# Opening of a diffusion step on one core: modulation weights loaded in column quarters, first five projections run over k in four passes

## What is computed

```
m = silu(cvec) @ w_ada + b_ada            # w_ada is 1024 x 6144, cvec: two vectors (context, latent)
sh1, sc1, g1, sh2, sc2, g2 = split(m, 6)  # each 1024 wide
h = rmsnorm(x) * norm_mix * (1 + sc1) + sh1
p = h @ w_in                              # w_in is 1024 x 3600, split into mq mk mv mo gate dq dk dv
```

## Time and profile before

| | |
|---|---|
| median of 3 runs | 712.12 us (709.15 to 714.17) |
| profiled execution, its own time | 710.51 us |
| its span | 708.6 us |
| PE busy | 663.3 us, 94% |
| DVE, ACT, POOL busy | 52%, 23%, 13% |
| mean granted TensorE clock | 0.982 |
| HBM traffic | 255 GB/s over the span |

### The profile page before, as it was taken

How to read it: one execution, slowest core, us unless ns; L and a number is a source line. 1 busy time by engine, 2 the same in 40 slices (tenths; PEclk the granted TensorE clock), 3 DMA queues, 4 the chain that set the end, 5 groups by cost and what they waited for, 6 DMA issues and landing times.

```text
span 708.6 us, 7606 instructions
## 1 busy us (share of the span) xinstructions
PE 663.3 (94%) x2646; PEld 362.3 (51%) x2646; DVE 368.8 (52%) x748; ACT 160.2 (23%) x416; POOL 95.0 (13%) x120
## 2 busy tenths in 40 slices
PE   3799999999999999999999899996999999999993
PEld 3344474345556555577778654443744444444441
DVE  3315562431465655366645636857563445545477
ACT  6000210001222221136655703222200100000113
POOL 1042100112203201020322310121100000000040
PEclk9899999999999999999999999999999999999997
DMA  7988833913015569999952249414899999999573
GB/s 281 387 261 307 322 136 118 358 31 134 31 30 164 229 274 375 421 352 420 420 239 64 87 159 406 176 70 191 303 341 370 389 344 349 346 370 336 208 296 148
DMA packets 63621, 181.46 MB, mean 256 GB/s; under 512 B 5622, under 2 KB 19310, under 8 KB 59492
## 3 DMA queue, kind: packets, MB, share of 16 engines
q1 hardware_dynamic: 54088, 157.53, 61.1%
q0 software_dynamic: 4384, 12.48, 4.9%
q10 hardware_dynamic: 5116, 11.02, 4.0%
HBM read 122.71 MB, written 58.25 MB: 255 GB/s over the span
## 4 chain that ended last, share of the span: by engine, by line
PE 74%; DVE 8%; DMA 8%; SPq 5%; issue 3%; ACT 1%; ACTq 0%; POOL 0%; DVEq 0%; POOLq 0%
PE PS L1645 24%; PE PS L2050 10%; PE PS L1878 7%; PE PS L1637 5%; PE PS L1793 5%; SPq L529 4%; PE PS L2070 4%; DMA RING<-scratch_xs 3%; PE PS L1865 2%; PE PS L1676 2%; DMA PR<-in_w_ada 2%; DMA PR<-scratch_mod 1%; PE PS L1772 1%; PE PS L1586 1%; PE PS L1822 1%
## 5 line engine op out<-in xcount | busy, mean ns | idle before, releaser
L1645 PE MATMUL PS<-RING,hT 128*128 128x512 f32 x400 | 180.7, 600 | 0.8 <-DVE hT L1053 0.8
L1645 PEld LDWEIGHTS PS<-RING,hT 128*128 128x128 f32 x400 | 73.6, 191 | 86.6 <-issue 85.6
L2050 PE MATMUL PS<-PR,RING 128*128 128x512 f32 x192 | 85.3, 593 | 0.6 <-DVE RING L1424 0.6
L1878 PE MATMUL PS<-RING,hT 128*128 128x512 f32 x160 | 72.7, 600 | 0.0
L2050 PEld LDWEIGHTS PS<-PR,RING 128*128 128x128 f32 x192 | 35.7, 190 | 41.4 <-issue 40.7
L1878 PEld LDWEIGHTS PS<-RING,hT 128*128 128x128 f32 x160 | 29.0, 190 | 30.5 <-issue 30.5
L2070 PE MATMUL PS<-PR,TMP 128*128 128x512 f32 x96 | 43.2, 592 | 0.0
L1793 PE MATMUL PS<-RING,hT 128*128 128x256 f32 x160 | 36.9, 384 | 0.7 <-ACT TMP L860 0.6
L1637 PE MATMUL PS<-hT,RING 128*128 128x512 f32 (+3 forms) x128 | 37.1, 450 | 0.0
L949 ACT ACTIVATE TMP<-PS 128x256 f32<-128x256 f32 x16 | 6.1, 384 | 131.5 <-PE PS L2050 131.5
L1030 DVE TENSOR_TENSOR TMP<-PS,TMP 2x512 f32<-2x512 f32 x24 | 16.4, 682 | 36.8 <-PE PS L1676 32.1
(11 more groups left out here) (345 smaller groups left out, 950.0 us busy)
## 6 DMA issues: line engine op xcount, KB each, us to landing
scratch_xs<-fnorm SPq DMA_DIRECT2D x16, 2560.0 KB, 23.6
PR<-in_w_gate_up SPq DMA_DIRECT2D x12, 2048.0 KB, 19.9
PR<-in_w_ada SPq DMA_DIRECT2D x20, 1024.0 KB, 10.4
RING<-in_w_in SPq DMA_DIRECT2D x14, 1024.0 KB, 7.5
PR<-in_w_down SPq DMA_DIRECT2D x12, 1024.0 KB, 23.3
hT<-in_w_gate_up SPq DMA_DIRECT2D x4, 2048.0 KB, 21.8
RING<-scratch_xs SPq DMA_DIRECT2D x56, 128.0 KB, 15.1
scratch_xs<-RING ACTq DMA_DIRECT2D x14, 512.0 KB, 12.5
```

The source lines that it names most:

```text
L1645: last = mm(PS[:, bank, :], hTv[:, k, t * P:(t + 1) * P], ring[:, ci % 2, k, :], start=(k == 0), stop=(k == KD - 1))
L1878: last = mm(PS[:, i % 4, :], hTv[:, k, t * P:(t + 1) * P], ring[:, (WOUT + q) % 2, k, :], start=(k == 0), stop=(k == KD - 1))
L2050: last = mm(PS[:, 4 + b, :], xgT[:, b, k, :], gub[s][:, k, :], start=(k == 0), stop=(k == KD - 1))
```

## The change

Each of the four modulation chunks now holds 256 columns of shift and the 256 columns of scale that belong to the same features; one chunk is enough to modulate two k blocks. `QUARTER` says which quarter of the features chunk n_ holds (0, 2, 1, 3 for n_ = 0, 1, 2, 3; in the order of PE, chunks 0, 2, 1, 3, the quarters are 0, 1, 2, 3). A transfer of such a chunk is all 8 k blocks by 256 columns. The first half of the mk chunk is loaded before ada 2, the second before ada 3. `modulate1(c)` and `ada_cols(c)` work by quarters, and the first five projections run in four passes of two k blocks (`first_proj`). The other tiles still use `proj` by halves.

```
 load_ada1(n_):
-            for hf in range(2):
-                sp.dma_start(ada_w1[n_][:, 4 * hf:4 * hf + 4, :], w_late[hf, :, :, n_ * 512:(n_ + 1) * 512]
+            c = QUARTER[n_]
+            for s in range(2):
+                sp.dma_start(ada_w1[n_][:, :, 256 * s:256 * s + 256], w_first[:, :, D * s + 256 * c:D * s + 256 * c + 256]
...
         load_ada1(0)
+        load_chunk(0, (0,))
         load_ada1(2)
-        load_chunk(0, (0,))
         load_ada1(1)
+        load_chunk(0, (1,))
         load_ada1(3)
-        load_chunk(0, (1,))
...
-        pool.dma_start(TMP[ROWS4 - 1:ROWS4, 2048:4096], bias[0:2048].unsqueeze(0)).then_inc(early_loaded, 16)
+        for s in range(2):
+            pool.dma_start(adp[ROWS4 - 1:ROWS4, :, 256 * s:256 * s + 256],
+                           bias[D * s:D * s + D].rearrange("(c n) -> c n", c=4).unsqueeze(0)).then_inc(early_loaded, 16)
...
+        def modulate1(c):
+            dve.wait_ge(ada_done, c + 1)
+            V.tensor_copy(adp[0:ROWS4 - 1, c, :], PS[0:ROWS4 - 1, 4, :]).then_inc(ada_row, 1)
+            dve.wait_ge(adacol_T, c + 1)
+            V.tensor_copy(modc[:, 2 * c:2 * c + 2, :], PS[:, 6, 4 * c:4 * c + 4].rearrange("p (k c) -> p k c", c=2))
+            step(V.scalar_tensor_tensor(modc[:, 8 + 2 * c:10 + 2 * c, :], ...
+            if c == 0:
+                dve.wait_ge(hraw_a, NT)
+                dve.wait_ge(hraw_v, NT)
+            for r, (lo, hi) in enumerate(((0, CTX), (CTX, T))):
+                for k in range(2 * c, 2 * c + 2):
+                    V.tensor_scalar(hTv[:, k, lo:hi], hTv[:, k, lo:hi], modc[:, 8 + k, r:r + 1], modc[:, k, r:r + 1],
+                                    ALU.mult, ALU.add).then_inc(h_ready, 1)
...
         ada(0, 0)
         xn_T(4)
-        pe.wait_ge(early_loaded, 48)
-        ada_cols(0, 0)
-        ada(2, 1)
-        ada_cols(2, 1)
+        pe.wait_ge(early_loaded, 64)
+        ada_cols(0)
...
+        def first_proj(m, c):
+            if m < 4 and c == 0:
+                pe.wait_ge(hraw_a, NT)
+                pe.wait_ge(hraw_v, NT)
+            if m == 0 and c % 2 == 0:
+                halves(0, c // 2)
+            for k in range(2 * c, 2 * c + 2):
+                if m < 2:
+                    pe.wait_ge(h_ready, 4 * c + 2 * m + k % 2 + 1)
+                last = mm(PS[:, FIRST_BANK[m], :], hTv[:, k, m * P:(m + 1) * P], ring[:, 0, k, :],
+                          start=(k == 0), stop=(k == KD - 1))
+            if c == 3:
+                last.then_inc(mm_done, 1)
...
-        proj(0, 0)
-        proj(1, 0)
+        for m in range(NT):
+            first_proj(m, 0)
+        ada(2, 1)
+        ada_cols(1)
+        for m in range(3):
+            first_proj(m, 1)
         ada(1, 2)
-        proj(2, 0)
-        ada_cols(1, 2)
+        first_proj(3, 1)
+        first_proj(4, 1)
+        ada_cols(2)
+        for m in range(3):
+            first_proj(m, 2)
         ada(3, 3)
-        proj(3, 0)
-        ada_cols(3, 3)
-        proj(4, 0)
+        first_proj(3, 2)
+        first_proj(4, 2)
+        ada_cols(3)
         for m in range(ALONE * NT):
             w, t = WIN_ORDER[m // NT], m % NT
             if m >= NT:
                 proj(m, 0)
-            proj(m, 1)
+                proj(m, 1)
+            else:
+                first_proj(m, 3)
             if m == 0:
                 gates()
```

More of the change, by code:

```diff
@@ L51 @@
 FIRST_BANK = (2, 3, 0, 1, 5)
+QUARTER = (0, 2, 1, 3)
 ADA2_AT = {4: 1, 5: 2, 6: 3, 7: 8, 8: 9, 9: 10, 10: 11, 11: 12}
@@ L429, in _ @@
             sp.dma_start(x_in[:, t, :], src).then_inc(x_loaded[t], 16)
+        w_first = a["w_ada"][0].rearrange("(k p) n -> p k n", p=P)
         w_late = a["w_ada"][0].rearrange("(h k p) n -> h p k n", h=2, p=P)
@@ L433, in load_ada1 @@
             done = (late_in[0], None, late_in[1], ada3_in)[n_]
-            for hf in range(2):
-                sp.dma_start(ada_w1[n_][:, 4 * hf:4 * hf + 4, :], w_late[hf, :, :, n_ * 512:(n_ + 1) * 512]
-                             ).then_inc(half_in[2 + hf] if n_ == 1 else done, 16)
+            c = QUARTER[n_]
+            for s in range(2):
+                sp.dma_start(ada_w1[n_][:, :, 256 * s:256 * s + 256], w_first[:, :, D * s + 256 * c:D * s + 256 * c + 256]
+                             ).then_inc(half_in[2 + s] if n_ == 1 else done, 16)
         load_ada1(0)
+        load_chunk(0, (0,))
         load_ada1(2)
-        load_chunk(0, (0,))
         load_ada1(1)
+        load_chunk(0, (1,))
         load_ada1(3)
-        load_chunk(0, (1,))
         def load_ada2(n_):
@@ L1035, in ada_rows @@
             last.then_inc(ada_row, 1)
[L1037 to L1048, removed]
+        def modulate1(c):
[3 more added lines that the diff above has]
+            V.tensor_copy(modc[:, 2 * c:2 * c + 2, :], PS[:, 6, 4 * c:4 * c + 4].rearrange("p (k c) -> p k c", c=2))
+            step(V.scalar_tensor_tensor(modc[:, 8 + 2 * c:10 + 2 * c, :],
+                                        PS[:, 6, 16 + 4 * c:20 + 4 * c].rearrange("p (k c) -> p k c", c=2), 1.0,
+                                        cols[:, 16 + 2 * c:18 + 2 * c].unsqueeze(2).broadcast_to([P, 2, 2]), ALU.add, ALU.mult))
+            if c == 0:
                 dve.wait_ge(hraw_a, NT)
                 dve.wait_ge(hraw_v, NT)
-            for c, (lo, hi) in enumerate(((0, CTX), (CTX, T))):
-                for k in range(4 * hf, 4 * hf + 4):
-                    V.tensor_scalar(hTv[:, k, lo:hi], hTv[:, k, lo:hi], modc[:, 8 + k, c:c + 1], modc[:, k, c:c + 1],
+            for r, (lo, hi) in enumerate(((0, CTX), (CTX, T))):
+                for k in range(2 * c, 2 * c + 2):
+                    V.tensor_scalar(hTv[:, k, lo:hi], hTv[:, k, lo:hi], modc[:, 8 + k, r:r + 1], modc[:, k, r:r + 1],
                                     ALU.mult, ALU.add).then_inc(h_ready, 1)
-        modulate1(0)
-        modulate1(1)
+        for c in range(4):
+            modulate1(c)
         V.memset(gzero, 0.0)
@@ L1580, in ada @@
             for k in range(KD):
-                if n_ == 1 and k % 4 == 0:
-                    pe.wait_ge(half_in[2 + k // 4], 16)
+                if n_ == 1 and k == 0:
+                    pe.wait_ge(half_in[2], 16)
+                    pe.wait_ge(half_in[3], 16)
                 elif k == 0:
@@ L1588, in ada, with ada_cols @@
             last.then_inc(ada_done, 1)
-        def ada_cols(n_, ci):
-            pe.wait_ge(ada_row, ci + 1)
+        def ada_cols(c):
+            pe.wait_ge(ada_row, c + 1)
             for j in range(4):
-                o = 2 * (4 * n_ + j)
-                last = mm(PS[:, 6, o:o + 2], adp[:, n_, j * P:(j + 1) * P], misc[0:ROWS4, 40:42], start=True, stop=True)
+                o = 16 * (j // 2) + 2 * (2 * c + j % 2)
+                last = mm(PS[:, 6, o:o + 2], adp[:, c, j * P:(j + 1) * P], misc[0:ROWS4, 40:42], start=True, stop=True)
             last.then_inc(adacol_T, 1)
@@ L1623, in proj @@
             ci = c
-            bank = FIRST_BANK[m] if m < NT else m % 2
-            if m >= NT and hf == 0:
+            bank = m % 2
+            if hf == 0:
                 pe.wait_ge(mm_evac, m - 1)
-            if m < 4 and hf == 0:
-                pe.wait_ge(hraw_a, NT)
-                pe.wait_ge(hraw_v, NT)
             if t == 0:
@@ L1642, in proj @@
             for k in range(4 * hf, 4 * hf + 4):
-                if m < 2:
-                    pe.wait_ge(h_ready, 8 * hf + 4 * m + k % 4 + 1)
                 last = mm(PS[:, bank, :], hTv[:, k, t * P:(t + 1) * P], ring[:, ci % 2, k, :],
```

## The result

The changed kernel takes 718.83 us (median of 4 runs, 716.90 to 721.18) against 710.63 us of the kernel before in the same comparison (4 runs): ratio 1.014, 95% interval 1.0095 to 1.0185. It is slower by about 8 (the two medians) to 10 us (the ratio). The forecast was 715.7 us, 3.6 us slower, with a chance of 0.88 for no more than 1%. Its profiled execution took 717.29 us with a span of 715.5 us, 6.9 more than before.

What follows compares the result with a forecast made beforehand. PE, busy in 94% of the span, was taken as the bound. Start -4.5, moved work with gaps and clock +5.6, waits +0.8 and +1.5, rounding +0.2 gave +3.6: 715.7 us, range 711.5 to 720.

Steps and rivals of the forecast that it cites:

- Step 1: Modulation chunk loads: 1 KB pieces move at 354 GB/s, so chunk 0 lands 0.50 us later.
- Step 2: Opening: ada 2 and its ada_cols leave the front, so the first projection starts at 25.8, 4.5 us earlier.
- Step 3: First projection to gates: moved work, 3.1 us of new gaps, 1.2 of low clock; gates end at 69.3.
- Step 4: Behind the gates: PE waits 0.8 and 1.5 us at the second and third ada2; mq starts at 86.1.
- First term: Gate rows through POOL behind the gates: 0.3 + 2.0 us to issue, some 2 to land, at 77.1.
- Second term: Chunk 6's load, issued at 73.4 when ada2(4) ends: each half lands 8.1 us after issue, at most 9.2.
- The upper end of 83.1: Latest landing of chunk 6 behind the gates, from a range of 82.0 to 83.1.
- pace is not lost: Behind the gates: the 2.3 us of waits go, leaving +1.1 to +1.4, 713.3 us; chance 0.25.
- Slow pieces: Chunk loads: 1 KB pieces move at only 217 GB/s, chunk 0 lands 4.24 later; +7.3, 719.4 us; chance 0.12.
- The low clock: Opening: the clock stays low for a second stretch, +1.7 us on the forecast, 717.4 us; chance 0.1.

Runs made afterwards that it cites:

- e3: Changed kernel, with SP issuing chunk 6's load only after the four gate-row transfers have landed; 719.58 us, ratio 1.0136 to the kernel before.
- e2: Changed kernel, with a tile's pass in front of and behind each of the three later ada_cols; 714.07 us, ratio 1.0057 to the kernel before.
- e5: Changed kernel run once more, unedited; 720.54 us, ratio 1.015 to the kernel before.
- e1: Changed kernel, with DVE waiting for the transferred gate rows one tile later, behind ada_rows(5); 717.46 us, ratio 1.0102 to the kernel before.

## Why the prediction was wrong

Step 1, the loads: the rate was right. 1 KB pieces onto 128 partitions move at 350 GB/s (354 on the line between 512 B and 2 KB; 1 KB onto 32 partitions had shown 217). The Trainium skill, "SBUF — State Buffer", section "Door 1: The DMA port swizzle", gives 32 partitions half of the ports that 128 have, and led the right way. The 512 B for line rate of the Trainium skill, "DMA: Bandwidth & Descriptors", section "Specifications", does not hold here, 350 at 1 KB against 387 at 2 KB. Chunk 0 was 0.8 later than before and not 0.5, and about 1 us over all traces.

Step 2, the start: right, 26.11 for 25.8 in this execution. With it came luck: the other four traces with the same opening start at 26.55 to 28.27, and the kernel before at 28.62 to 33.36, so a single pair of traces can't test 4.5 us. The start won less than step 3 cost, as forecast.

Step 3, the moved work: right. The gates end at 70.04 for 69.3, 0.7 late, of which 0.3 was there at the start; gaps 0.81 and 0.70, 0.80, 0.70 us for 0.77 and three of 0.79; a low clock of 3 to 4 us from 26 us on, which cost 1.7 us in the first pass for 1.2.

Step 4 is the step that failed, in the size of its terms. The two mechanisms, DVE's rows queued behind the wait for the gate rows and chunk 6's load hanging on the end of ada2(4), were named and are both real, but the wait in front of ada2(6) was put at 1.5 us and measured 4.97 and 4.28. First term: "some 2 to land" for the gate rows, from a row where nothing else moved, in a place where I had myself let chunk 6's load be issued at the same time (73.4); they took up to 6.4 (e3 shows 1.9 without the load). Second term: 8.1 us for the landing of both halves, the median of the earlier trace rows; PE needs the last half, and that took 9.7 (9.1 before). The upper end of 83.1 was too low by that, 84.5. Third: no clock price for the wait. The clock fell within these 5 us of idling and cost 2.4. It was so after the waits of 3.56 (e2), 4.28 (e5) and 5.61 us (e3) too, with an ada2 of 3.26, 2.65 and 3.52 us for 1.90, and not after e1's 2.91. With 5.0 + 2.4 for 1.5 the sum would have been +9.5 (3.6 + 3.5 + 2.4), against a measured 8 to 10. In the trace, mq starts 6.9 us later than forecast (93.01 for 86.1): 3.5 and 2.4 of it by these terms, 0.7 from before the end of the gates, and the rest is rounding in the lengths of blocks. The places of all of it were in the text.

The rivals: "pace is not lost" is refuted, it was lost by more. Slow pieces are refuted by 350 GB/s. The low clock came, but in another place than I had put it (behind the long wait; a second low stretch in the opening did not come in this trace, but it did in e1, e3 and e5, in the second pass, and cost 1.4 to 1.7 us, which is the rival's 1.7; so it is a matter of the execution). The chance for no more than 1% was too high because every term of step 4 was taken from the quiet end or the middle of its row, and they are not independent: the load that PE waits for also delays the gate rows, and the wait brings the low clock.

## What to carry to other kernels

When matmuls are moved from behind a point to before it, what stands behind it is squeezed: look for loads, small transfers and rows of other engines that hang on an event there, count their full round trip (here 10.2 us from the end of ada2(4) to chunk 6), and compare it with the PE work that is left (7 us). A small transfer's latency from a quiet moment does not hold once a big load is issued in the same microsecond; take the one measured beside a load, and the last half, not the median. Before an early start costs nothing, the later users of a buffer have to be moved back by as much work as was taken from in front of them. And ask what the start saves: work that is only moved is no gain, and here, with the waits and most of the gaps taken away, the time was even with the kernel before.

## What was not expected of the hardware

Transfers of 10 KB from SBUF to SBUF, four of them on POOL's queue, landed in 1.9 us alone and in up to 6.4 us beside a 2 MB load of SP's queue. The first small loads (`misc`, SP) end PE's first wait at 5.8 to 6.0 us in the four traces of the kernel before and its variants and at 6.6 to 7.4 in the eight of the changed one; the extra bias transfer on POOL is something that all eight have and none of the four, but it was not tried by itself. The low stretches of the granted clock (0.50) in the opening begin and end at other times in each execution, and were most of what moved the first projection of one and the same kernel by 3 us (30.37 and 33.36; the first 1.0 us of it is chunk 0's landing).
